# A two-layer hybrid encoder: TensorE's flag read in the expert stage, high-part gathers first, another first order of the queue, and an output in four pieces

## The reference, cut to what is computed

```python
for i in range(DEPTH):                       # DEPTH = 2
    h = rms_norm(x, norm1_g[i])
    q, k, v, z, xbc, dt_raw, gate_a, gate_m = split(h @ w_in[i])
    ya = diff_attention(...) @ w_attn_out[i]       # 8 heads, two softmax maps each
    ym = ssd_mixer(...) @ w_ssm_out[i]             # bidirectional scan, 32 heads
    x = x + (sigmoid(gate_a) * ya + sigmoid(gate_m) * ym) @ w_out[i]
    hn = rms_norm(x, norm2_g[i])
    # hierarchical mixture: best group of 4, best 2 of its 8 experts, no token dropped
    x = x + hier_moe(hn, ..., w_exp_gate[i], w_exp_up[i], w_exp_down[i])
# one expert: (silu(xb @ w_gate) * (xb @ w_up)) @ w_down, d = 1024, ff = 512, 32 experts a layer
```

## Time and profile before

| | |
|---|---|
| median of 3 runs | 1877.91 us (1877.11 to 1878.66) |
| the profiled execution | 1878.55 us, its span 1876.8 us |
| mean granted TensorE clock | 0.987 |
| busy share: PE, DVE, ACT, POOL | 93%, 38%, 37%, 35% |
| chain of waits by engine | PE 77%, DVE 12%, ACT 5%, issue 4% |
| read from HBM | 525.82 MB, mean 281 GB/s |
| packets of the queue q8 (instruction) | 78, of 1.28 MB in all |

### The profile page before, as it was taken

The page is one execution under the profiler, slowest core; times in us unless marked ns, Lnnn a source line. Parts: engine busy times, 40 slices in busy tenths (PEclk is TensorE's granted clock), DMA queues, the critical chain, the costliest instruction groups (busy, mean ns, idle before and its releaser), DMA issues.

```text
span 1876.8 us, 23441 instructions
## 1 busy us (share of the span) xinstructions
PE 1741.8 (93%) x9076; PEld 1084.5 (58%) x9076; DVE 710.8 (38%) x1350; ACT 686.1 (37%) x1521; POOL 654.8 (35%) x534
## 2 busy tenths in 40 slices
PE   7999999999999998889889999999999999988987
PEld 5879776786444343343358897767864444343432
DVE  4518677523222121221255186784242222221211
ACT  4565577754111111111145656676541111111111
POOL 6688655795000000000056886657950000000000
PEclk9999899999999999999999999999999999999999
DMA  6544311446899999999934443114568999999996
GB/s 243 186 162 163 128 46 45 180 195 244 350 420 427 427 428 428 428 427 429 397 121 167 175 162 113 46 51 174 213 243 364 428 428 427 428 427 428 427 427 260
DMA packets 39734, 528.51 MB, mean 282 GB/s; under 512 B 4248, under 2 KB 7064, under 8 KB 7872
## 3 DMA queue, kind: packets, MB, share of 16 engines
q1 hardware_dynamic: 39584, 526.89, 68.4%
q0 software_dynamic: 32, 0.02, 0.0%
HBM read 525.82 MB, written 1.06 MB: 281 GB/s over the span
## 4 chain that ended last, share of the span: by engine, by line
PE 77%; DVE 12%; ACT 5%; issue 4%; POOL 1%; DMA 1%; SPq 0%; DVEq 0%; ACTq 0%
PE PS L1057 24%; PE PS L1088 12%; PE PS L730 7%; PE PS L732 7%; PE PS L731 7%; DVE view L1638 4%; PE PS L1038 3%; PE PS L1023 2%; PE PS L855 2%; PE PS L1024 2%; PE PS L886 1%; DVE view L1634 1%; DVE view L1843 1%; PE PS L718 1%; DVE view L1906 1%
## 5 line engine op out<-in xcount | busy, mean ns | idle before, releaser
L2005 POOL TENSOR_TENSOR view<-view,view 128x512 fp32r<-128x512 f32 x448 | 576.7, 1309 | 656.2 <-DVE view L1540 493.1
L1057 PE MATMUL PS<-view,view 128*64 128x512 f32 x2048 | 454.6, 598 | 45.8 <-issue 45.7
L1057 PEld LDWEIGHTS PS<-view,view 128*64 128x64 f32 x2048 | 158.4, 138 | 336.1 <-issue 336.0
L1177 ACT ACTIVATE view<-view 128x512 fp32r<-128x512 f32 x448 | 274.4, 630 | 203.1 <-PE PS L732 192.9
L730 PE MATMUL PS<-view,view 128*128 128x512 f32 x704 | 297.4, 422 | 9.6 <-POOL view L2005 8.1
L731 PE MATMUL PS<-view,view 128*128 128x512 f32 x704 | 276.3, 392 | 0.0
L732 PE MATMUL PS<-view,view 128*128 128x512 f32 x704 | 276.1, 392 | 0.0
L1088 PE MATMUL PS<-view,view 128*64 128x512 f32 x1024 | 228.5, 599 | 0.3
L1898 DVE TENSOR_TENSOR view<-PS,view 128x512 f32<-128x512 f32 x32 | 22.1, 692 | 423.0 <-PE PS L1057 423.0
L730 PEld LDWEIGHTS PS<-view,view 128*128 128x128 f32 x704 | 133.5, 190 | 48.4 <-issue 15.1
L731 PEld LDWEIGHTS PS<-view,view 128*128 128x128 f32 x704 | 133.8, 190 | 32.6 <-issue 8.2
(11 more groups left out here) (240 smaller groups left out, 2068.8 us busy)
## 6 DMA issues: line engine op xcount, KB each, us to landing
view<-in_w_exp_gate_dram SPq DMA_DIRECT2D x64, 2048.0 KB, 23.3
view<-in_w_exp_up_dram SPq DMA_DIRECT2D x64, 2048.0 KB, 26.2
view<-in_w_exp_down_dram SPq DMA_DIRECT2D x64, 2048.0 KB, 27.1
view<-in_w_mix_dram SPq DMA_DIRECT2D x56, 2048.0 KB, 7.8
view<-bias_table SPq DMA_DIRECT2D x2, 1536.0 KB, 11.9
view<-in_x_dram SPq DMA_DIRECT2D x1, 1024.0 KB, 5.0
out_dram<-view SPq DMA_DIRECT2D x1, 1024.0 KB, 5.5
dtw<-in_w_dt_dram SPq DMA_DIRECT2D x2, 256.0 KB, 11.6
```

The lines of the kernel that those rows point to most:

```text
L1057: ins = pe.matmul(bank(ph, name, j)[e * CAP:(e + 1) * CAP, :], xgT2[h % 2][:, k, at + e * CAP:at + (e + 1) * CAP], slot8[expert_block(j, k ...
L1177: nc.scalar.activation(highs(chunk), weights(slot8, chunk), ACT.Copy).then_inc(*high_ready.up(ph))
L2005: g_.tensor_tensor(weights(low8, chunk), weights(slot8, chunk), highs(chunk), ALU.subtract).then_inc(*low_ready.up(ph))
```

## The change

- **Start.** The token rows are first in the queue. Only the channel columns stay ahead of blocks 0 to 2; the shared row, the router and the dt weights follow block 2. `small_in` now counts two loads, and the new `columns_in` one. ACT copies the bias table after the two squares, PE waits for that copy after its filler and not before it, and DVE computes the head scales after the low parts of the transposed rows. Layer 1's filler has 26 products, not 28.
- **Router.** DVE makes ranks and selection first and then `XNl`, each half with a signal of its own. PE has 5 filler products there, not 10, and the first gather runs all 16 high-part products first, then the low parts of the first 128 tokens, then of the second. ACT and DVE copy the gathered banks before anything about the gates. The gate product of an even pair waits for each gathered bank where it first needs it.
- **Flag.** PE reads it after the down product of pair 8. The jump stays at the end of the layer.
- **Output.** Four DMAs of 256 KB, each behind its own addition.

```diff
@@ sync
+            sp.dma_start(X, x.rearrange("b (t p) d -> p (b t) d", p=P)).then_inc(s_x, 16)
             sp.dma_start(rel[:, :], rel_bias).then_inc(s_rel, 16)
             sp.dma_start(oh.rearrange("p a b -> p (a b)"), onehot_dram).then_inc(s_rel, 16)
-            sp.dma_start(X, x.rearrange("b (t p) d -> p (b t) d", p=P)).then_inc(s_x, 16)
+            def channel_vectors(l, ph):
+                sp.dma_start(vcols[l][:, :], columns[ds(l, 1)].rearrange("a p c -> p (a c)")
+                             ).then_inc(*columns_in.up(ph))
...
+                    if l == 0 and i == RING - 1:
+                        vectors(0, ph)
...
-            for b in (5, 6):
-                sp.wait_ge(*drained[b].at(end, 0))
-            sp.dma_start(out.rearrange("b (t p) d -> p (b t) d", p=P), X).then_inc(s_out, 16)
-            sp.wait_ge(s_out, 16)
+            for t in range(TT):
+                for n in range(2):
+                    cols = slice(n * COLS, (n + 1) * COLS)
+                    sp.wait_ge(*out_of(Phase(DEPTH - 1), "s", ALL_PAIRS - 1, t, n))
+                    sp.dma_start(rows[:, t, cols], X[:, t, cols]).then_inc(s_out, 16)
+            sp.wait_ge(s_out, 16 * 2 * TT)
@@ tensor
-            pe.wait_ge(s_tabc, 1)
...
-                keep_busy(28 if l else 24)
+                keep_busy(26 if l else 24)
+                if l == 0:
+                    pe.wait_ge(s_tabc, 1)
...
-                keep_busy(10)
-                first_pass(ph)
-                pe.wait_ge(*flag_ready.at(ph, 1))
-                pe.sem_inc(s_anchor, 1)
-                over = pe.value_load(flag[0:1, 0:1], min_val=0, max_val=1)
+                keep_busy(5)
+                over = first_pass(ph)
                 with pe.If(over > 0):
...
+                def first_gather(i, t, part):
+                    for k in (2 * i, 2 * i + 1):
+                        ins = pe.matmul(bank(ph, "xg", 0, i)[:, (k % 2) * HALF:(k % 2 + 1) * HALF],
+                                        part[:, t, k * P:(k + 1) * P], S2[0][:, t, :],
+                                        start=(part is XNh and t == 0 and k % 2 == 0),
+                                        stop=(part is XNl and t == TT - 1), skip_group_check=True)
+                    return ins
+                pe.wait_ge(*xnh_ready.at(ph, 1))
+                pe.wait_ge(*S_ready.at(ph, 1))
+                for i in range(4):
+                    pe.wait_ge(*free(ph, "xg", 0, i))
+                    for t in range(TT):
+                        first_gather(i, t, XNh)
                 pe.wait_ge(*xnl_ready.at(ph, 1))
                 for i in range(4):
-                    gather(0, i)
+                    first_gather(i, 0, XNl)
+                pe.wait_ge(*xnl_ready.at(ph, 2))
+                for i in range(4):
+                    first_gather(i, 1, XNl).then_inc(*fill(ph, "xg", 0, i))
...
+                            if kind == 0 and j % 2 == 0 and k % 2 == 0:
+                                pe.wait_ge(*out_of(ph, "xg", h, k // 2))
...
+                    if j == ALL_PAIRS // 2:
+                        pe.wait_ge(*flag_ready.at(ph, 1))
+                        pe.sem_inc(s_anchor, 1)
+                        over = pe.value_load(flag[0:1, 0:1], min_val=0, max_val=1)
```

More of the change, by code:

```diff
@@ L644, in layer @@
                         if not last:
+                            channel_vectors(l + 1, Phase(l + 1))
                             vectors(l + 1, Phase(l + 1))
@@ L683, in unit @@
                     pair(ph, j)
-            vectors(0, Phase(0))
+            channel_vectors(0, Phase(0))
             for l in range(DEPTH):
                 layer(l, l == DEPTH - 1)
-            end = Phase(DEPTH)
-            for b in (5, 6):
-                sp.wait_ge(*drained[b].at(end, 0))
-            sp.dma_start(out.rearrange("b (t p) d -> p (b t) d", p=P), X).then_inc(s_out, 16)
-            sp.wait_ge(s_out, 16)
+            rows = out.rearrange("b (t p) d -> p (b t) d", p=P)
+            for t in range(TT):
[4 more added lines that the diff above has]
+            sp.wait_ge(s_out, 16 * 2 * TT)
         @block.tensor
@@ L1196, in layer @@
                                          accum_out=small[:, t:t + 1]).then_inc(*sumsq.up(ph))
+                if l == 0:
+                    act.wait_ge(s_tab, 1)
+                    nc.scalar.activation(rtab.rearrange("p a b -> p (a b)"), PS[0:HEADS, 7, :], ACT.Copy
+                                         ).then_inc(s_tabc, 1)
                 cast(ph, 0, HIGHS)
-                act.wait_ge(*small_in.at(ph, 3))
+                act.wait_ge(*columns_in.at(ph, 1))
                 for k in range(KD):
@@ L1788, in layer @@
                 v.tensor_tensor(maskh[:, :, :], rt[:, 2], rt[:, 5], ALU.add).then_inc(*mask_ready.up(ph))
-                dve.wait_ge(*xnh_ready.at(ph, 1))
-                for t in range(TT):
-                    ins = v.scalar_tensor_tensor(out=XNl[:, t, :], in0=X[:, t, :], scalar=r_row[:, t:t + 1],
-                                                 in1=XNh[:, t, :], op0=ALU.mult, op1=ALU.subtract)
-                ins.then_inc(*xnl_ready.up(ph))
                 dve.wait_ge(*full(ph, "rank"))
@@ L1848, in layer @@
                 select(0)
+                dve.wait_ge(*xnh_ready.at(ph, 1))
+                for t in range(TT):
+                    v.scalar_tensor_tensor(out=XNl[:, t, :], in0=X[:, t, :], scalar=r_row[:, t:t + 1],
+                                           in1=XNh[:, t, :], op0=ALU.mult, op1=ALU.subtract
+                                           ).then_inc(*xnl_ready.up(ph))
                 v.tensor_tensor(rs4[:, 0], gl, wide(gmax, GROUPS), ALU.subtract).then_inc(*soft.up(ph))
```

34 lines of the change are left out of this document (15 added, 19 removed).

## The result

The changed kernel took 1865.76 us (median of 4 runs, 1865.48 to 1867.73) against 1878.22 for the kernel before beside it (4 runs, 1877.11 to 1878.66): a ratio of 0.9935, with a 95% interval of 0.9924 to 0.9947, or 12.5 us less. The forecast was 1861.8 with a range of 1856.0 to 1867.5; about three quarters of its 16.1 us came. The profiled execution is the slowest of the four, 1867.73 with a span of 1866.0.

A forecast was written before the change was run, and what follows sets the result against it. It took the weight stream to bound the expert stages, with gains ahead of them and at program ends and layer joint; 3.1 + 5.3 + 3.6 + 1.9 + 2.2 = 16.1 us gave 1861.8, range 1856.0 to 1867.5.

The forecast's parts named there:

- Bound of the stages: Expert stages: the weight stream sets the pace but stalls at 480 to 482 us, so an earlier gate product advances the stage.
- The second rival: Expert stages don't start earlier as a whole, so the gathers' 8.9 us are lost: 1870.7 us; chance 0.06.
- Start, 3.1: Program start: earlier block 0 and casts bring the first product 2.0 us forward, plus 1.1 from the clock; bounds 1.0 to 4.5.
- less what the table's inputs lose by standing behind the rows: Program start: unsized deduction from the fillers' starting some 0.6 us earlier without the wait for ACT's table copy.
- Gather, 5.3 and 3.6: First gather: earlier selection and copies bring the gate product 3.6 us forward per layer; layer 0 5.3 us with the clock.
- The 1.7 of the clock: Layer 0's first gate product: the shorter pause ahead of it avoids the low clock, saving 1.7 us.
- Flag, 1.9: End of layer 0: moving PE's flag read gains 1.1 us, two fewer fillers 0.8; bounds 1.1 to 4.5.
- I take 1.1 on PE: End of layer 0: the flag read makes 1.1 of PE's 4.97 us idle time; the rest is the jump.
- the first rival: End of layer 0: the idle time was the read, not the jump; 7.8 us gained, time 1855.9; chance 0.10.
- Output, 2.2: Program end: the last quarter store lands sooner than one 1 MB DMA's 5.5 us, gaining 2.2 us; bounds 1.8 to 3.3.
- The clock's, 1865.2: With half the fillers PE runs the first gate product or joint at 1.2 GHz, 1.7 us at two places; chance 0.11.
- The start's, 1864.5: Program start: the queue lands block 0 no earlier, so the start doesn't move; time 1864.5; chance 0.05.

The follow-up runs named there:

- x_table_first: Changed kernel with the table's two small loads ahead of the token rows in SyncE's queue again: 1865.35 us (6 runs).
- x_vec_first: Changed kernel with the small vectors (shared row, router and step weights) issued before the first weight block again, rows still first: 1868.6 us (5 runs).
- u_gather_all: Changed kernel with the whole gather as before the change, including its order on PE, DVE and ACT: 1873.23 us (8 runs).
- x_fill_first: Changed kernel with the 26 fillers at the joint of the layers put ahead of PE's branch instead of behind it: 1859.15 us (4 runs).
- u_out: Changed kernel with the output written in one 1 MB transfer behind the last sum again: 1866.83 us (6 runs).

## Why the prediction was right or wrong

The time fell inside the range, 4.0 us above the forecast. The places and the mechanisms were mostly right, and four sizes were too large. Term by term, in the prediction's order:

- **Bound of the stages: right.** The stream still stood at 0.02 from 480 to 482, SyncE issued at 481.12 instead of 487.09, and layer 0 ended 5.68 earlier. Gains ahead of a stage pass through it. The second rival is refuted.
- **Start, 3.1: mis-sized, 1.9.** The failing step is "less what the table's inputs lose by standing behind the rows". I gave it no number, though the rows had one: X is 1 MB, and what follows waits for its bytes. The map took 2.9 us longer to land (4.68 against 1.8), and the table product started 1.1 later, more than the 0.7 of the wait for ACT's copy that was saved. The fillers gate the transposes, so it came through, and the first product came at 18.6 on the mean and not at 17.5. With the table's loads in front it came at 17.11 (x_table_first). The mechanism of the block and the casts was right (0.5 in x_vec_first), and so was the saving at the clock, 1.0 for the 1.1 named. 1.9 is the mean of ten profiles at 42 us, against the one of before; the start was not undone as a whole, and a late block can take part of it away again (x_table_first).
- **Gather, 5.3 and 3.6: right in mechanism, 7.3 by the runs.** The 3.6 a layer are there in both layers (3.67, 3.68), and by u_gather_all they are all of the 7.3. The 1.7 of the clock was named in the right place, but booked as sure. With the old pause of 2.06 to 2.10 and more, the clock fell in 4 of 6 places, with the new one in none of 20; but the clock also fell behind the scan in most profiles, with the old gather as with the new. The profile of before shows it there in layer 1, and I had not looked. A fall there is as large as the difference between the 10.8 of the two spans and the 12.5 of the medians, but no profile of the other runs shows that it is the reason.
- **Flag, 1.9: about right in sum, 1.6, by luck, with a step that failed.** That step is "I take 1.1 on PE", by SyncE's 0.9. On PE the read costs nothing that the idle time shows (4.79 with it, 4.90 without). SyncE's 0.9 was taken between two issues of an engine that does nothing else, which is likely why it does not carry over. What came, came from two fewer fillers and from how long the clock stayed low in them: the joint took 14.6 to 16.5 us in nine profiles that have the branch ahead of the fillers, on the mean 15.3, against 16.8 in the one profile of before. The reading that the rest is the branch was right, with 4.9 in place of 3.9, and it refutes the first rival, that the read was all of it; what that rival priced at 7.8 us could be had by other means, 6.8 in x_fill_first.
- **Output, 2.2: 2.1 between the two profiles, 0.9 by the runs.** The term went by one transfer whose 5.5 was the longer of two (4.3 in the other). The upper bound of 3.3 was not worked out either: 5.0 less its 2.45 is 2.55, not 2.2, and the quarter's own bytes come on top. The Trainium skill (DMA: Bandwidth & Descriptors, Anatomy of one DMA) gives its fit for DMAs that GpSimd issues, and these are SyncE's; its estimates, 4.4 and 2.6, are near the 4.3 of u_out and the 2.6 of the quarters, and not near the 5.5 of before.
- **Rivals.** The clock's, 1865.2: the clock stayed up in the gate product and fell elsewhere, behind the scan. The start's, 1864.5 (by the term of 3.1 it should have been 1864.9): the block did land earlier, cast from 11.72. The time came out within 1.3 us of both, for reasons that neither named, so it tells nothing in their favour.

The measured terms make 1.9 + 7.3 + 1.6 + 0.9 = 11.7 of 12.5 us. The 0.8 left over is within what medians and single profiles scatter here. Only the 7.3 is clear of that scatter by itself: 1.9 and 1.6 are means of traces against a single one of before, and 0.9 lies between overlapping runs.

## What to carry to other kernels

Before you shorten an idle stretch, find which instruction in it costs, and test the neighbours: the read was moved, the branch behind it was the price, and work handed to the engine ahead of the branch hid it and gained 6.8 us. A small load behind a large one in a queue lands with the large one, so ask of each what it gates. And pieces of a chain belong together: XNl's place put back by itself cost 6.8 us, though it delays the gather by only 3.8, and the exponentials left in the new place cost 8.8 once the copies were back in the old.

## What the runs showed of the hardware

- A branch on PE that skips a large body cost 4.6 to 5.0 us of idle time in all ten profiles that had it bare, with an instruction packet 2.3 us behind the last product in the changed kernel; with 5.79 us of matmuls ahead of it, nothing, and the packet came while they ran.
- The granted clock fell to 0.50 behind pauses of 1.1 to 2.1 us in some executions and not in others of the same program. A fall cost 1.6 to 1.7 us, in a kernel whose times spread over 4 us.
- 24 fillers from an idle PE took 6.56 to 8.10 us in ten profiles of the same start.
- The same 1 MB store took 5.5 and 4.3 us from issue to landing, and a 64 KB load 1.8 to 2.0 us in front of the 1 MB row load and 4.5 to 4.9 behind it.
- The same 2 MB weight block of the mixer was cast 7.5 to 9.5 us after its issue in fourteen profiles.
